# Output projections read by rows of their weights, three quarters of them placed between attention units

## What is computed

```python
# block 1: gated recurrence (4 heads), sparse attention (4 heads), convolution
mix = jnp.concatenate([o_a, o_b, o_c], axis=-1) @ w_out[l]
x = x + g1 * mix
h = rmsnorm(x, norm_mlp_w[l]) * (1.0 + sc2) + sh2
# block 2, layer 0: MLA (8 heads) and stick-breaking attention (8 heads)
return jnp.concatenate([o_a, o_b], -1) @ w_out
# block 2, layer 1: forgetting attention (16 heads)
return o @ w_out
# both layers
x = layer_norm(DEEPNORM_ALPHA * x + mix, ln1_g[i], ln1_b[i])
```

## Time and profile before

| | |
|---|---|
| runs | 1313.17, 1294.94, 1300.74 us; median 1300.74 |
| profiled execution | span 1301.2 us from the first to the last instruction; it has no other time of its own |
| PE matmul, PE weight load, DVE, ACT busy | 89%, 81%, 58%, 42% |
| mean granted TensorE clock | 0.936 of full |
| stretch of the dsa stage with its projection | from the end of the first convolution half, about 215, to the scaling of `xn`, 298.35 us |
| stretch of mla with its projection | 609.8 to 661.2 us |
| stretch of fox units 8 to 15 with their projection | 1003.2 to 1063.2 us |

### The profile page before, as it was taken

How to read it: one execution, slowest core, us unless ns; L and a number is a source line. 1 busy time by engine, 2 the same in 40 slices (tenths; PEclk the granted TensorE clock), 3 DMA queues, 4 the chain that set the end, 5 groups by cost and what they waited for, 6 DMA issues and landing times.

```text
span 1301.2 us, 19178 instructions
## 1 busy us (share of the span) xinstructions
PE 1159.6 (89%) x8196; PEld 1057.0 (81%) x8196; DVE 756.3 (58%) x940; ACT 548.4 (42%) x762; POOL 0.2 (0%) x4
## 2 busy tenths in 40 slices
PE   4879888598999998965889999998999889999997
PEld 2879777388998878964789999887988589999887
DVE  2574557655775455357576566476453567566557
ACT  4562326344343334365543333344445544333333
POOL 0000000000000000000000000000000000000000
PEclk8788999888999997987889999998999999999999
DMA  9523661323555544420135555534522034455550
GB/s 386 228 87 117 267 254 70 130 90 107 193 184 181 193 159 181 172 77 1 66 130 183 176 193 186 191 143 176 197 98 97 1 132 180 177 193 174 193 184 33
DMA packets 29092, 200.98 MB, mean 154 GB/s; under 512 B 3152, under 2 KB 4688, under 8 KB 5840
## 3 DMA queue, kind: packets, MB, share of 16 engines
q1 hardware_dynamic: 27440, 190.30, 40.1%
q10 hardware_dynamic: 1568, 9.46, 1.9%
HBM read 198.70 MB, written 1.05 MB: 154 GB/s over the span
## 4 chain that ended last, share of the span: by engine, by line
PE 75%; DVE 12%; ACT 6%; DMA 5%; issue 2%; SPq 0%; DVEq 0%; ACTq 0%
PE bank L545 22%; PE bank L550 21%; PE bank L551 21%; DMA raw<-wstream 4%; DVE w_lo L1444 3%; PE bank L702 2%; ACT w_hi L1055 1%; DVE hT_lo L1462 1%; PE bank L695 1%; PE bank L961 1%; PE bank L785 1%; PE bank L620 1%; PE bank L960 1%; PE bank L637 1%; PE bank L669 1%
## 5 line engine op out<-in xcount | busy, mean ns | idle before, releaser
L1444 DVE TENSOR_TENSOR w_lo<-raw,w_hi 128x2048 fp32r<-128x2048 f32 (+1 forms) x159 | 358.3, 2257 | 185.5 <-ACT w_hi L1055 179.4
L1055 ACT ACTIVATE w_hi<-raw 128x2048 fp32r<-128x2048 f32 (+1 forms) x159 | 299.5, 1886 | 294.4 <-PE bank L545 251.3
L545 PE MATMUL bank<-hT_hi,w_hi 128*128 128x256 f32 (+1 forms) x1360 | 392.7, 289 | 17.7 <-DVE w_lo L1444 10.1
L550 PE MATMUL bank<-hT_lo,w_hi 128*128 128x256 f32 (+1 forms) x1360 | 390.5, 287 | 0.0
L551 PE MATMUL bank<-hT_hi,w_lo 128*128 128x256 f32 (+1 forms) x1360 | 390.2, 287 | 0.0
L545 PEld LDWEIGHTS bank<-hT_hi,w_hi 128*128 128x128 f32 (+1 forms) x1360 | 264.8, 195 | 21.7 <-DVE w_lo L1444 11.1
L550 PEld LDWEIGHTS bank<-hT_lo,w_hi 128*128 128x128 f32 (+1 forms) x1360 | 264.8, 195 | 0.5
L551 PEld LDWEIGHTS bank<-hT_hi,w_lo 128*128 128x128 f32 (+1 forms) x1360 | 264.6, 195 | 0.6
L545 PE MATMUL bank<-w_hi,hT_hi 128*128 128x256 f32 (+2 forms) x544 | 159.6, 293 | 23.4 <-DVE w_lo L1444 13.0
L550 PE MATMUL bank<-w_lo,hT_hi 128*128 128x256 f32 (+2 forms) x544 | 157.6, 290 | 0.0
L551 PE MATMUL bank<-w_hi,hT_lo 128*128 128x256 f32 (+2 forms) x544 | 157.6, 290 | 0.0
(11 more groups left out here) (268 smaller groups left out, 1107.0 us busy)
## 6 DMA issues: line engine op xcount, KB each, us to landing
raw<-wstream SPq DMA_DIRECT2D x179, 1024.0 KB, 4.8
arena<-prow ACTq DMA_DIRECT2D x2, 2560.0 KB, 10.4
x_res<-x ACTq DMA_DIRECT2D x1, 1024.0 KB, 15.0
rows<-prow ACTq DMA_DIRECT2D x2, 512.0 KB, 23.6
out<-x_res SPq DMA_DIRECT2D x4, 256.0 KB, 2.1
const_sb<-const ACTq DMA_DIRECT2D x1, 872.0 KB, 19.1
raw<-wstream SPq DMA_DIRECT2D x1, 768.0 KB, 4.4
raw<-wstream SPq DMA_DIRECT2D x1, 544.0 KB, 3.7
```

The source lines that it names most:

```text
L545: ins = mm(o, a[0], b[0], start=start, stop=False)
L550: mm(o, a[0], b[1], start=False, stop=False)
L1055: A(w_hi[n % HI][:, 0:m], raw[:, slot % RAW, 0:m], ACT.Copy).then_inc(weights_rounded, 1)
L1444: V.tensor_tensor(w_lo[slot][:, 0:m], raw[:, slot, 0:m], w_hi[n % HI][:, 0:m].bitcast(F32), ALU.subtract).then_inc(weights_split, 1)
```

## The change

The output projection of each of the three stages is cut the other way. A tile now holds two chunks of input channels (one pair) and all 1024 output columns, and the products of a stage add up in four banks, one for each 128 positions x 512 columns. SP gathers such a tile from the four tiles of the stream, so the weights in memory stay as they are. Three of the four row tiles are done inside the attention: PE's order has row halves (one chunk, four blocks, 12 matmuls of 128x512) between the units, and only the fourth tile comes after the last unit.

```diff
-def unit_order(name, n):
+def unit_order(name, n, rows=()):
...
+        order += [("rows", pair, half) for step, pair, half in rows if step == i]
     return order
+ROW_STAGES = {"wo": (0, 1, 3, 2), "o0": (2, 3, 0, 1), "o1": (0, 1, 2, 3)}
+DSA_ROWS = [(1, 0, 0), (1, 0, 1), (1, 1, 0), (1, 1, 1), (5, 3, 0), (6, 3, 1)]
+MLA_ROWS = [(2, 2, 0), (3, 2, 1), (4, 3, 0), (6, 3, 1), (8, 0, 0), (9, 0, 1)]
+FOX_ROWS = [(9, 0, 0), (10, 0, 1), (12, 1, 0), (13, 1, 1), (16, 2, 0), (17, 2, 1)]
...
+UNIT_BANKS, ROW_BANKS = (4, 5, 6, 7), (0, 1, 2, 3)
...
-    plan.extend([("conv", c) for c in range(2)])
-    plan.append(("cmean",))
-    plan.extend([("mod", 10), ("mod", 11)])
-    plan.append(("cvar",))
-    plan.extend([("ms", 10), ("ms", 11)])
-    plan.extend([("hgt", 0), ("hgt", 1)])
-    plan.extend(unit_order("dsa", 4))
+    plan.extend([("conv", 0), ("mod", 10), ("mod", 11), ("conv", 1), ("cmean",), ("hgt", 0), ("hgt", 1), ("cvar",),
+                 ("ms", 10), ("ms", 11)])
...
+                if name in ROW_TILES:
+                    stage, pair = ROW_TILES[name]
+                    base = min(TILE_NO[row_name(stage, q)] for q in range(4))
+                    sp.dma_start(raw[:, i % RAW, :].rearrange("p (j n) -> p j n", j=4),
+                                 wstream[base:base + 4, :, pair * 512:(pair + 1) * 512].rearrange("j p n -> p j n"))\
+                        .then_inc(weights_loaded[i % RAW], 16)
+                    continue
...
+            def row_half(stage, pair, half):
+                pairs = ROW_STAGES[stage]
+                if stage not in opened:
+                    opened.append(stage)
+                    for t, n in blocks:
+                        begin(stage, t, n)
+                    chunks(DC, pairs)
+                if half != 1:
+                    row_tiles[stage, pair] = tile(row_name(stage, pair))
+                    x_ready(2 * pair)
...
+                for i, t, n in order:
+                    k = 2 * pair + i
+                    o = psum[bank(stage, t, n)].rearrange("p (b n) -> p b n", b=2)
+                    stop = half is None and i == 1
+                    last = product3(o, x_part(k, t * P, (t + 1) * P), (vh[:, n, :, i, :], vl[:, n, :, i, :]),
+                                    pair == pairs[0] and i == 0, stop, first)
...
-            chunks(DC, (0, 1, 3, 2))
-            gemm_token("wo0", True)
-            gemm_token("wo1")
+            row_half("wo", 2, None)
```

Units of the three stages (in fox from unit 8 on) now use banks 4 to 7 alone, banks 0 to 3 hold the sums. ACT and DVE round and split a row tile inside the attention as well, where before they did so after it. DVE's places:

```diff
+                    if i in tiles:
+                        lo_ahead(tiles[i], 0)
                     if 0 <= i - 3 < n:
                         unit_output(name, us, i - 3, c0)
...
-            lo_ahead("hi.1", 1)
+            lo_ahead("hi.1", 2)
...
-                    {0: [(0, 0)], 1: [(1, 0)], 2: [(3, 0)]})
+            softmax("dsa", 4, 0, lambda t: sel_bias[t][:, 0:(t + 1) * P], 0.125, 4, {1: [(3, 0)]},
+                    {3: "wo1.0"})
...
-                            {1: [(2, 0)], 2: [(3, 0)], 7: [(0, 4)]})
+                            {1: [(2, 0)], 2: [(3, 0)], 7: [(0, 4)]}, {5: "o0_1.0", 8: "o0_1.1"})
...
-                            {12: [(0, 4)], 13: [(1, 8)], 15: [(2, 12)]})
+                            {8: [(0, 4)], 11: [(1, 8)], 15: [(2, 12)]},
+                            {9: "o1_0.1", 12: "o1_1.0", 16: "o1_1.1"})
```

More of the change, by code:

```diff
@@ L151, in fox_order @@
             order.append(FOX_UPPER[i - 1])
+        order += [("rows", pair, half) for step, pair, half in FOX_ROWS if step == i]
     return order
@@ L218, in psum_plan, with beside_rows @@
     plan.extend([("hgo", 0), ("hgo", 1)])
-    plan.extend([("conv", c) for c in range(2)])
-    plan.append(("cmean",))
-    plan.extend([("mod", 10), ("mod", 11)])
-    plan.append(("cvar",))
-    plan.extend([("ms", 10), ("ms", 11)])
-    plan.extend([("hgt", 0), ("hgt", 1)])
-    plan.extend(unit_order("dsa", 4))
-    gemm("wo0")
-    gemm("wo1")
+    plan.extend([("conv", 0), ("mod", 10), ("mod", 11), ("conv", 1), ("cmean",), ("hgt", 0), ("hgt", 1), ("cvar",),
+                 ("ms", 10), ("ms", 11)])
+    within(range(BANKS))
+    def beside_rows(stage, order):
+        for key in order:
+            if key[0] != "rows":
+                one(key, UNIT_BANKS)
+        for i, (t, n) in enumerate([(t, n) for t in range(TT) for n in range(2)]):
+            plan.append((stage, t, n))
+            banks_of.append(ROW_BANKS[i])
+    beside_rows("wo", unit_order("dsa", 4, DSA_ROWS))
     transposes("mlp")
@@ L253, in psum_plan @@
             plan.append(("fd",))
-            plan.extend(fox_order())
-        gemm(f"o{layer}_0")
-        gemm(f"o{layer}_1")
+            order = fox_order()
+            first = order.index(("fox", "L", 8))
+            plan.extend(order[:first])
+            within(range(BANKS))
+            beside_rows("o1", order[first:])
         transposes(f"ln1_{layer}")
@@ L670, in decay_level, with attention @@
                     last.then_inc(psum_full, 1)
-            def attention(name, heads, logits, values, probs, base, order=None):
+            blocks = [(t, n) for t in range(TT) for n in range(2)]
+            opened, row_tiles = [], {}
+            def row_half(stage, pair, half):
[8 more added lines that the diff above has]
+                    x_ready(2 * pair)
+                wh, wl, first = row_tiles[stage, pair]
+                vh, vl = (w.rearrange("p (h b k n) -> p h b k n", h=2, b=2, k=2) for w in (wh, wl))
+                order = [(i, t, n) for t, n in blocks for i in range(2)] if half is None else [
+                    (half, t, n) for t, n in blocks]
+                for i, t, n in order:
[4 more added lines that the diff above has]
+                                    pair == pairs[0] and i == 0, stop, first)
+                    if stop:
+                        last.then_inc(psum_full, 1)
+            def attention(name, heads, logits, values, probs, base, order=None, stage=None):
                 us = units(heads)
                 for key in order or unit_order(name, len(us)):
+                    if key[0] == "rows":
+                        row_half(stage, key[1], key[2])
+                        continue
                     if key in FOX_UPPER:
@@ L1224, in _ @@
             ahead("hi.1", 2)
+            b = wait_full("conv", 1)
+            done(A(conv[:, T:2 * T], b[:, 0:T], ACT.Identity, bias=col("cv_b", 1)), "conv", 1)
+            warm_root(15)
             act.wait_ge(bank_read[bank("cvar")], read("cvar"))
@@ L1230, in _, with residual_squares @@
             last.then_inc(conv_sig_done, 1)
-            softmax("dsa", 4, 0)
-            for n, n_ in enumerate(("wo0.0", "wo0.1", "wo1.0", "wo1.1")):
-                ahead(n_)
-                if n == 3:
-                    warm_root(3)
-                act.wait_ge(x_res_ready, n + 1)
-                for t in range(TT):
-                    s = slice(n * T, (n + 1) * T)
-                    last = A(xn[:, t, s], x[:, t, s], ACT.Square, accum_out=ssum[:, 4 * t + n:4 * t + n + 1])
-            last.then_inc(squares_summed, 1)
+            row_tile_at = {1: "wo0.0", 4: "wo0.1"}
+            softmax("dsa", 4, 0, lambda i: ahead(row_tile_at[i]) if i in row_tile_at else None)
+            def residual_squares(first):
+                for i in range(4):
+                    act.wait_ge(x_res_ready, first + i + 1)
+                    s = slice(i % 2 * 512, (i % 2 + 1) * 512)
+                    last = A(xn[:, i // 2, s], x[:, i // 2, s], ACT.Square, accum_out=ssum[:, i:i + 1])
+                last.then_inc(squares_summed, 1)
+            ahead("wo1.1")
+            warm_root(3)
+            residual_squares(0)
             square_root(TT, 3, False)
@@ L1352, in _ @@
                         done(A(qT_a[0:96, j * 512:(j + 1) * 512], b[0:96, :], ACT.Copy), "qt", j)
-                    softmax("mla", 8, base)
+                    row_tile_at_0 = {4: "o0_0.0", 7: "o0_0.1"}
+                    softmax("mla", 8, base, lambda i: ahead(row_tile_at_0[i]) if i in row_tile_at_0 else None)
                     base += 8
@@ L1383, in _ @@
                     base += 16
[L1384 to L1386 removed]
+                ahead(f"o{layer}_1.1")
                 roots += 1
@@ L1497, in rms_norm, with softmax @@
                 own(xn_ready, TT)
-            def softmax(name, heads, base, bias, scale, c0, beside):
+            def softmax(name, heads, base, bias, scale, c0, beside, tiles):
                 us = units(heads)
```

141 lines of the change are left out of this document (66 added, 75 removed).

## The result

| | before | with the change |
|---|---|---|
| median (lowest to highest), runs | 1313.07 us (1294.94 to 1317.50), 20 | 1298.59 us (1292.14 to 1301.13), 20 |
| profiled execution: span, mean granted clock | 1301.2 us, 0.936 | 1299.3 us, 0.934 |

The account below looks back on a forecast made before the run. PE was taken to bound the kernel, with three quarters of the span; gains of 12 us in dsa and 3 in mla less 1 in fox make 14, from 1301.2 (profile; median 1300.74) to 1287, range 1274 to 1299.

Parts of the forecast that it names:

- Shape: Output projections: 96 matmuls of 512 columns at 0.2267 us replace 192 of 256; 1.3 us less per stage.
- Ahead of dsa: Before dsa's units: the new order brings the first logits 8.3 us earlier, at 246.9; PE waits for the second gate row.
- dsa, -12: Stage dsa: head start and partly filled waits, with 4 us of slow clock, gain 12 us; scaling at 286.1.
- mla, -3: Stage mla: row halves fill part of PE's idle time and shorten the slow clock, a net gain of 3 us.
- fox, +1: Stage fox, second half: row halves fill no idle time and roundings cost 0.8, a net loss of 1 us.
- Costed at nothing: Gathered loads of 512 pieces of 2 KB, and four banks for the units: both taken to cost no time.
- The base: Starting time of the whole kernel: profiled execution 1301.2 us, median of the runs 1300.74, from which 14 us were taken.
- Only the head start: Rival: conversions moved into the softmax lengthen the loop in all three stages; gain only 1 to 5 us, 1298; chance 0.18.
- The rows fill: Rival: PE in the attentions has neither idle nor slow stretches; gain 29 us, 1272; chance 0.10.
- Held by the four banks: Rival: logits wait for a unit's bank, six tiles each delay the loop by 4.2 us; 25 us more, 1312; chance 0.07.
- late gathered loads: Rival: a gathered load takes 19 us and holds ACT's second convolution copy; 10 to 15 us lost, 1300; chance 0.03.
- The prediction's own sign of being wrong: Matmuls of 512 columns off 0.227, PE waiting for DMA at a row tile, or mla and fox together moving over 8 us.

Follow-up runs that it names:

- e4: The change with six row halves moved one or two steps later, two in mla and four in fox: 1277.81 us, ratio 0.9741.
- e7: The change with row tiles packed in memory by the host, so loads are 128 pieces of 8 KB: 1297.01 us, ratio 0.9907.
- e2: The change with the row halves of all three stages, and their conversions, behind the last unit: 1295.37 us, ratio 0.9900.
- e3: The change with row halves between the units in dsa only, those of mla and fox behind the last unit: 1298.76 us, ratio 0.9912.
- e12: The kernel before, unchanged, a single profiled execution that fell in the upper group of its times: 1317.53 us.
- e11: e4 plus gate rows in banks 6 and 7, dsa's halves spread over steps 1 to 3, fourth tile's second half split earlier: 1267.60 us, ratio 0.9692.

## Why the forecast of 1287 was wrong

The median lies 0.4 us inside the range. That the medians are 14.5 apart, and 14 was forecast, is luck: the 14 was counted from 1301, and from there the change gains 2 to 3.

- **Shape.** Right: 0.2267 us for 512 columns in the row tiles too. By the Trainium skill ("TensorE: Matmul & The Clock Gate", Back-to-back issue gap) N/2.4 + 2.5 ns, its formula for an isolated gap, would give an estimate of 0.216; the trace doesn't agree. A row half costs 2.86 and not 2.72, since its first matmul stands 0.34 ahead of the second (e4, 611.14 to 614.00).
- **Ahead of dsa.** Right: first logits 8.6 us earlier, against 8.3, and PE held by the second gate row.
- **dsa, -12.** It gave -8.6. The slow stretch at the start lasted 5 us and not 4, and I had seen only that one. Behind the row tiles came waits of 1.94 and 1.03, and with them the second (0.73 over 11.6 us), through the chain of units 2 and 3. Less the 3.0 of the later start, the 48 matmuls ended 0.9 later than forecast, the last tile began 3.7 later (279.8, forecast 276.1) and so did the scaling (289.8, forecast 286.1). What is left, 8.6, is the head start alone: the filling gave nothing.
- **mla, -3.** It gave -0.2. The waits were right: 3.2 + 2.8 + 1.7 forecast, 3.2 + 2.7 + 1.9 measured. Wrong was "with the row halves in it PE works without a break and I take 4, which is worth 3". The low clock did shrink, from some 10 us to 7. But it used to lie on units that wait for ACT and DVE anyway, and now lies on two row halves, which are PE-bound and take 1.3 and 1.6 us more each than at full clock (4.16 and 4.46). That eats the 3. That the units paid little for it before is argued; no run takes it apart.
- **fox, +1.** It gave +8.8. "I fill nothing" was exactly right (4.9 before and after), but "16.3 + 0.8 + 1.75 + 5.4 - 23.2 = +1" has no term for the clock at all, and fox had 13 more us at 1.2 GHz. **This is the step that failed**: the clock's loss in fox, put at nothing more than before had, both for the row halves and last tile behind waits that stay and for the units. 3.5 of the missing 7.8 lie behind the start of the first row half (56.5 us to mark e before, 61.0 in the change): the half behind the wait of 2.75 took 4.4 us and the last tile 7.3 instead of 5.4, behind a wait of 2.1 instead of 1.75. The other 4.3 lie ahead of it, where PE's instructions in fox are those of before (d to the same place takes 66.1 before and 70.4 in the change), in a stretch whose clock can have either level. e4, which moves six halves and changes nothing else, is 20 us shorter in mla and fox, of which the same 4.3 are a part.
- **Costed at nothing.** Right for the gathered loads (e7; 0.3 us longer each, and hidden) and for the four banks: no wait of PE for a unit's bank shows in mla or fox.
- **The base.** Wrong. Of the three runs shown one stood 12 us over the others, and I took median and profile for the kernel's one level. They were the lower of two. Against the lower group the change gains 3 us (1301.6 to 1298.6), against the upper 16.5. In none of its 20 runs does the change reach the upper group; a likely reason is that the row halves end the slow stretches of fox: the fall behind the wait of 1.09 is over as soon as the first row half runs, and there fox takes 131.3 in both profiles (change and e7), where without row halves the low clock came back for 27 us and fox took 134.6 to 136.1 (e2, e3, e12). That link is argued, not shown.
- **The rivals.** "Only the head start", 1298, has the right time, and the head start is indeed all that dsa gained, but the reason is wrong: e4 has the same conversions inside the softmax and is 21 us faster. "The rows fill", 1272, is not what this change does; e4 and e11 show that it was to be had, with other places. "Held by the four banks" and "late gathered loads" fell. The prediction's own sign of being wrong, mla and fox together moving by more than 8 us, came: they moved by 8.6.

What stays open: why the clock of the same instructions falls in one execution and holds in the next.

## What to carry to other kernels

Work moved from behind a stage into it belongs in the engine's waits or ahead of them; right behind a wait of 2 to 3 us it ran at 1.2 GHz for some 3 us, and PE-bound work pays that in full. So list what stands behind each wait that stays, and price it at 1.2 GHz. Before a base is chosen, look whether the runs of the kernel before form groups: a spread of 18 us in three runs was larger than the effect.
